# One more pair of block products in the v projection of a two-block network: the third group of 1024 columns splits its turns as the second and fourth do

## The reference, cut to what matters

```
h = rmsnorm(x, a_norm)                       # 256 x 2048
z = h @ a_w_in                               # 2048 x 12288, split into u | v | gate, 4096 columns each
v = rmsnorm(gelu(v), a_v_gain)
sv = einsum(w_s, v) + b_s                    # mixes the tokens of a chunk of 128
x = x + (u * sv * silu(gate)) @ a_w_out
```

## Time and profile before

| | us |
|---|---|
| median of 3 runs (2103.09 to 2103.61) | 2103.13 |
| the profiled execution | 2102.89 |
| its span | 2101.1 |
| PE busy in the span | 2095.3 |
| DVE busy | 1504.5 |
| ACT busy | 1112.8 |
| second, third and fourth group of v on PE | 52.19 to 93.0, 93.34 to 135.5, 135.6 to 176.4 |

### The profile page before, as it was taken

How to read it: one execution, slowest core, us unless ns; L and a number is a source line. 1 busy time by engine, 2 the same in 40 slices (tenths; PEclk the granted TensorE clock), 3 DMA queues, 4 the chain that set the end, 5 groups by cost and what they waited for, 6 DMA issues and landing times.

```text
span 2101.1 us, 25230 instructions
## 1 busy us (share of the span) xinstructions
PE 2095.3 (100%) x10012; PEld 1753.5 (83%) x10012; DVE 1504.5 (72%) x1690; ACT 1112.8 (53%) x1314; POOL 17.5 (1%) x17
## 2 busy tenths in 40 slices
PE   9999999999999999999999999999999999999999
PEld 7888888888888887888888888888888888888887
DVE  7987656665787754554669677877777777779986
ACT  6765444444456544554455454555555555555553
POOL 0000000000000000100000000000000000000000
PEclk9999999999999999999999999999999999999999
DMA  8665555555764655544465756556555556556663
GB/s 336 210 199 177 195 191 188 191 189 183 270 219 153 196 195 168 178 150 143 150 199 188 232 160 204 167 186 193 184 187 194 189 186 192 184 175 235 222 205 135
DMA packets 111957, 404.40 MB, mean 192 GB/s; under 512 B 12512, under 2 KB 13280, under 8 KB 111328
## 3 DMA queue, kind: packets, MB, share of 16 engines
q1 hardware_dynamic: 109440, 394.66, 57.5%
q10 hardware_dynamic: 2400, 8.14, 1.0%
HBM read 400.65 MB, written 2.10 MB: 192 GB/s over the span
## 4 chain that ended last, share of the span: by engine, by line
PE 96%; DVE 2%; ACT 1%; DMA 1%; issue 0%; ACTq 0%; DVEq 0%
PE g L555 37%; PE g L652 23%; PE xs L580 8%; PE g L580 8%; PE xs L675 5%; PE xs L584 4%; PE g L584 4%; PE g L679 4%; PE xs L603 1%; DVE w_lo L1432 1%; PE xs L833 1%; PE xs L712 1%; ACT w_hi L1014 0%; DMA raw<-in_stream 0%; PE xs L830 0%
## 5 line engine op out<-in xcount | busy, mean ns | idle before, releaser
L1432 DVE TENSOR_TENSOR w_lo<-raw,w_hi 128x1024 fp32r<-128x1024 f32 x659 | 803.6, 1224 | 498.9 <-ACT w_hi L1014 493.2
L1014 ACT ACTIVATE w_hi<-raw 128x1024 fp32r<-128x1024 f32 x659 | 697.5, 1059 | 757.5 <-PE g L555 412.4
L555 PE MATMUL g<-w_hi,mid_both 128*128 128x512 f32 x1024 | 326.5, 394 | 0.0
L555 PE MATMUL g<-w_hi,in_both 128*128 128x512 f32 x1024 | 318.6, 390 | 0.1
L555 PEld LDWEIGHTS g<-w_hi,in_both 128*128 128x128 f32 x1024 | 192.2, 188 | 40.2 <-DVE v_all L1564 0.5
L555 PEld LDWEIGHTS g<-w_hi,mid_both 128*128 128x128 f32 x1024 | 192.3, 188 | 39.5
L555 PE MATMUL g<-w_lo,mid_both 128*128 128x512 f32 x512 | 199.3, 389 | 0.0
L555 PE MATMUL g<-w_lo,in_both 128*128 128x512 f32 x512 | 199.2, 389 | 0.0
L580 PE MATMUL g<-mlp_both,w_hi 128*128 128x512 f32 x704 | 176.8, 393 | 0.0
L580 PE MATMUL xs<-mlp_both,w_hi 128*128 128x512 f32 x704 | 176.3, 392 | 0.0
L580 PEld LDWEIGHTS g<-mlp_both,w_hi 128*128 128x128 f32 x704 | 126.6, 189 | 22.8
(11 more groups left out here) (403 smaller groups left out, 3051.8 us busy)
## 6 DMA issues: line engine op xcount, KB each, us to landing
raw<-in_stream SPq DMA_DIRECT2D x659, 512.0 KB, 3.6
d_block<-in_stream SPq DMA_DIRECT2D x28, 512.0 KB, 5.0
o_block<-in_stream SPq DMA_DIRECT2D x24, 512.0 KB, 4.7
v_block<-in_stream SPq DMA_DIRECT2D x20, 512.0 KB, 4.4
gm_block<-in_stream SPq DMA_DIRECT2D x12, 512.0 KB, 5.7
x_first<-in_x_tokens ACTq DMA_DIRECT2D x2, 1024.0 KB, 6.8
gain_row<-in_gain_rows SPq DMA_DIRECT2D x8, 256.0 KB, 3.7
xt<-in_x_tokens ACTq DMA_DIRECT2D x1, 2048.0 KB, 8.1
```

The source lines that it names most:

```text
L555: ins = mm(G[buf][:, t, :], a[:, kt, at_t], w[:, slot, j * COLS:(j + 1) * COLS], start=(kt == 0 and n == 0), stop=(last and j == ROWS_PER_ ...
L1014: activation(w_hi[:, n % RING, :], of[:], ACT.Copy).then_inc(hi_ready, 1)
L1432: v.tensor_tensor(w_lo[:, n % RING, :], of, w_hi[:, n % RING, :].bitcast(F32), ALU.subtract).then_inc(lo_ready, 1)
```

## The change

The third group takes the table row of the second one: the chunks of turn 0 run with the products of turn 3, and those of turn 1 with the products of turn 2. Before, turns 0 and 2 were plain, and the chunks of turn 1 ran with the products of turn 3.

```
 WIDE_STEPS = {
     "v": (((0, None), (1, None), (2, None), (3, None)),
           ((0, 3), (1, 2)),
-          ((0, None), (1, 3), (2, None)),
+          ((0, 3), (1, 2)),
           ((0, 2), (1, 3))),
```

## The result

| | median us (runs) | against the kernel before |
|---|---|---|
| before | 2103.22 (6) | |
| changed | 2118.76 (6), 2118.59 to 2120.42 | ratio 1.0076, 95% interval 1.0065 to 1.0087 |
| profiled execution of the changed kernel | 2120.42, span 2118.4 | before: 2102.89, span 2101.1 |

A forecast was written before the change was run, and what follows sets the result against it. PE was taken as the bound; -1.36 us for matmuls, +6.21 and +6.63 for the two borders gave +11.5 us on the profiled 2102.89, and with the runs' median 0.24 higher 2114.6 us, range 2111 to 2122.

The forecast's parts named there:

- What bounds: Whole kernel: PE is the bound, busy 2095.3 of 2101.1 us, so each new PE wait costs its full length.
- Six matmuls less: Third group: one plain turn of 48 matmuls becomes one of 42, 1.36 us less.
- the whole sum: All terms together: -1.36 + 6.21 + 6.63 = +11.5 us.
- The border of groups 2 and 3: Start of third group: PE waits 6.56 us for `own_read` behind DVE's additions and block sums; net +6.21 us.
- The border of groups 3 and 4: Start of fourth group: same DVE chain and stall, +6.56 us, and +0.07 for the first matmul.
- DVE and ACT fit into the group: Third group: added DVE work (39.5 of 40.8 us) and three more ACT `w_hi` fit, costed at nothing.
- The clock: Behind each stall: TensorE taken at full 2.4 GHz, so no added time.
- the rival: Behind both stalls: the clock falls to 1.2 GHz, about +4 us, 2118.6 us, up to 2121.8; chance 0.34.
- No wait: Both borders: `own_read` comes in time, so each border is free, 2101.4 us; chance 0.04.
- Shorter chain: Both borders: block sums lie elsewhere in time, each stall 2.81 us, 2107 us; chance 0.07.
- DVE as the bound of the whole third group: Third group: slower block sums make DVE the bound, +1 to +3 us on the forecast, 2116 to 2118; chance 0.07.

The follow-up runs named there:

- experiment 3: Changed kernel with 28 matmuls that compute nothing of the result put ahead of the first product's wait at each of the two borders: 2114.55 us.
- Experiments 1 and 2: Kernel before with the third group's one mixed pair moved to first place (2111.29 us) or to last place (2111.52 us), same amount of work.
- Experiment 2: Kernel before with the third group's one mixed pair moved to last place: 2111.52 us, ratio 1.0042.
- experiments 4 to 7: Changed kernel with: early DVE additions (2107.51 us); narrower wait of the first product (2108.66); two chunks first (2106.98); that plus early additions and `v_all` (2104.78).
- 6: Changed kernel with two chunks ahead of the first product in groups 3 and 4, DVE's additions unmoved: 2106.98 us.
- 10: Changed kernel with two chunks ahead of the first product in groups 3 and 4, and ACT's gelu and squares later: 2103.59 us.
- experiment 11: Changed kernel with two chunks first in groups 3 and 4, later gelu and squares, earlier `v_all`, and early DVE additions in v alone: 2102.77 us.
- experiment 4: Changed kernel with all four DVE additions at the last P6 and one step behind it, ahead of the block sums: 2107.51 us.
- experiment 5: Changed kernel with the first product of groups 3 and 4 waiting only for ACT's copy of its own bank, not `own_read`: 2108.66 us.

## Why the prediction was right, and where not

- *What bounds.* Right. The lost 15.5 us are idle or slow time of PE in v; from `ug` on nothing changed (1924.5 us in both).
- *Six matmuls less.* PE has 10006 in place of 10012. Worth 1.36 us by the spacing of the matmuls. No run has this term alone; experiment 3 bears out the whole sum with it (+11.7 measured, +11.5 predicted).
- *The border of groups 2 and 3.* Right: 6.56 us predicted, 6.61 measured, each start on DVE within 0.01 us once the late start of the group is taken off. Experiments 1 and 2 show that the place of P1 does it. Of its two parts, the 2.81 us for the new place and the 3.75 for three block sums, no run has the first alone; the parts stand on the rows of DVE only.
- *The border of groups 3 and 4.* Right, 6.61 us. Experiment 2 has this stall alone.
- *DVE and ACT fit into the group.* Right for the changed kernel, where no further wait appeared behind the stalls. But as a statement on room it was too kind: 39.5 of 40.8 us leaves DVE so little that the order of its work decides, and experiments 4 to 7 ran into it at the next place each time. ACT, 30.2 of 40.8 us busy, which I costed at nothing, was worth 3.4 us when the products stood closer (6 against 10). Room counted over a group says little on a ring of four items.
- *The clock.* This is the step that failed. I took the full clock because a stretch of 1.1 us had left it at 1.00, and gave the fall a chance of 0.34. It fell in both stalls, so the forecast lacks this term, and the time lies in the range only because the range took in the rival. That rival's price was near: about +4 predicted, 4.2 measured by experiment 3 (3.9 by sessions). This was in part luck: it was the middle between no slow matmul and 18 behind each stall, 3.6 us for both stalls, rounded up, and no row stood behind that middle. The rule of the Trainium skill (TensorE: Matmul & The Clock Gate, Part 1: The HAM clock gate) that I had set beside it, that an idle TensorE goes to 1.2 GHz and is slow for a while when it works again, was what the chip did. My evidence was weaker than I said. The 1.1 us lie at the very start, ahead of PE's first matmul (it starts at 1.05), so they say nothing of a clock that falls after work; the next longest wait in the old trace's list is 0.4 us. And I read "full in all 40 slices" from nines that mean 90% or more; in windows of 2 us the old trace does show 1.00 over its first 14 us, but the page could not have told.
- *The rivals.* No wait: refuted by the two waits of 6.5 us. Shorter chain: refuted by DVE's starts. DVE as the bound of the whole third group: not in this kernel. The clock: it is the case that came.

What stays open: experiment 11 left DVE's `w_lo` as the limit of the second pair (the gap at P7), and no order of the items was tried that spreads that pair too.

## What to carry to other kernels

Before more work of a cheaper kind is put in a place where it has stood elsewhere, look at the instruction that comes first in it and at what it waits for: here a wait that every product had always carried was free behind a plain turn and cost 6.6 us behind a mixed one. Follow the waited-for engine's queue instruction by instruction from the last known start; with durations from the trace this gave each start to 0.01 us, and a second engine's share of busy time would not have shown it. And where a change makes PE stand for several us, add to the stall what the clock takes behind it, here 2 us each; of 1.36 us that the arithmetic promised nothing would have been left even with the border mended.

## What the runs showed of the hardware

- In two stalls of 6.6 us the granted clock fell to half 4.5 and 2.6 us after PE had gone idle, and was back 4.8 and 6.2 us after PE had begun to work again. Some 11 matmuls of 128x512 behind the first stall and some 14 behind the second ran 0.427 us apart in place of 0.227, which cost 2.3 and 3.0 us. The stalls of experiments 1 and 2, 6.6 us as well, show the same with other numbers: the clock fell 4.2 and 3.3 us after PE had gone idle and was back 4.4 and 3.5 us after P1. These are four samples of three executions.
- A wait of 1.8 us with 4 us of work between it and the next one of 0.3 (experiment 4), and three waits of 0.8 to 1.3 us within 8 us (experiment 5), left it at 1.00.
- A first matmul behind a wait has 0.07 to 0.11 us more to its successor than the others, even at the full clock, so many short waits cost more than the list of waits counts.
